# Bias matmuls of the experts in row groups of 32, and rest products by halves

## The reference, cut to what matters

```python
def expert_block(args):
    x_blk, e = args
    gu = x_blk @ w_gate_up[e] + b_gate_up[e]
    g = jnp.minimum(gu[:, :D_FF], SWIGLU_LIMIT)
    u = jnp.clip(gu[:, D_FF:], -SWIGLU_LIMIT, SWIGLU_LIMIT)
    act = (u + 1.0) * (g * jax.nn.sigmoid(SWIGLU_ALPHA * g))
    return act @ w_down[e] + b_down[e]
```

## Time and profile before

| | |
|---|---|
| time, median of 3 | 2289.41 us (2286.81 to 2292.16) |
| profiled execution: time | 2291.37 us |
| profiled execution: span, first to last instruction | 2289.70 us |
| mean granted TensorE clock | 0.982 |
| busy: PE, PE weight loads, DVE, ACT, POOL | 2181.7, 1690.9, 1607.8, 1325.1, 591.0 us |
| read from DRAM, written | 475.30 MB, 43.50 MB |

### The profile page before, as it was taken

How to read it: one execution, slowest core, us unless ns; L and a number is a source line. 1 busy time by engine, 2 the same in 40 slices (tenths; PEclk the granted TensorE clock), 3 DMA queues, 4 the chain that set the end, 5 groups by cost and what they waited for, 6 DMA issues and landing times.

```text
span 2289.7 us, 38734 instructions
## 1 busy us (share of the span) xinstructions
PE 2181.7 (95%) x13724; PEld 1690.9 (74%) x13821; DVE 1607.8 (70%) x1572; ACT 1325.1 (58%) x1484; POOL 591.0 (26%) x538
## 2 busy tenths in 40 slices
PE   7899999999898996999999999999999999999997
PEld 7877777677576874777787777787887777777775
DVE  4065757575466345887887887797998778777777
ACT  4166666666443113566676675676776556555665
POOL 1311101011165001143433432232332223222222
PEclk9999999999999997999999999999999999999998
DMA  4101202121265326998998998898998889888883
GB/s 147 28 28 47 74 26 67 35 67 62 78 206 204 111 84 261 358 344 280 339 347 286 337 353 280 309 375 298 403 368 296 294 294 337 277 291 287 307 313 113
DMA packets 267764, 515.66 MB, mean 225 GB/s; under 512 B 33541, under 2 KB 78032, under 8 KB 267692
## 3 DMA queue, kind: packets, MB, share of 16 engines
q1 hardware_dynamic: 241388, 471.38, 57.2%
q0 software_dynamic: 17088, 39.14, 7.3%
q10 hardware_dynamic: 9216, 4.20, 0.6%
HBM read 475.30 MB, written 43.50 MB: 227 GB/s over the span
## 4 chain that ended last, share of the span: by engine, by line
PE 57%; ACT 2%; DVE 1%; issue 1%; DMA 0%; POOL 0%; POOLq 0%; ACTq 0%; DVEq 0%
PE ex_gu L2112 30%; PE ex_yp L2160 15%; PE ex_rest L2134 4%; PE ex_rest L2177 3%; ACT ex_whi L1732 2%; PE ex_gu L2070 1%; PE ex_gu L2103 1%; PE ex_tr L2078 1%; PE ex_gu L2078 1%; PE ex_yp L2149 0%; DVE ex_wlo L1988 0%; PE ex_rest L2128 0%; PE ex_gu L2086 0%; PE ex_tr L2070 0%; DMA ex_xg<-xn_s,ex_idx 0%
## 5 line engine op out<-in xcount | busy, mean ns | idle before, releaser
L1988 DVE TENSOR_TENSOR ex_wlo<-ex_raw,ex_whi 128x2048 fp32r<-128x2048 f32 x387 | 876.6, 2291 | 217.2 <-ACT ex_whi L1732 217.2
L1732 ACT ACTIVATE ex_whi<-ex_raw 128x2048 fp32r<-128x2048 f32 x387 | 735.5, 1926 | 220.5 <-PE ex_gu L2112 152.0
L2112 PE MATMUL ex_gu<-ex_whi,ex_xhi 128*128 128x512 f32 x1024 | 290.5, 405 | 1.0 <-DVE ex_xlo L2029 1.0
L2112 PE MATMUL ex_gu<-ex_whi,ex_xlo 128*128 128x512 f32 x1024 | 275.3, 391 | 0.0
L2112 PE MATMUL ex_gu<-ex_wlo,ex_xhi 128*128 128x512 f32 x1024 | 274.6, 390 | 0.0
L2112 PEld LDWEIGHTS ex_gu<-ex_whi,ex_xhi 128*128 128x128 f32 x1024 | 191.8, 189 | 52.4 <-issue 7.4
L2112 PEld LDWEIGHTS ex_gu<-ex_whi,ex_xlo 128*128 128x128 f32 x1024 | 192.8, 188 | 41.6
L2112 PEld LDWEIGHTS ex_gu<-ex_wlo,ex_xhi 128*128 128x128 f32 x1024 | 192.8, 188 | 40.7
L705 POOL TENSOR_TENSOR at_wlo<-at_raw,at_whi 128x1024 fp32r<-128x1024 f32 x29 | 71.7, 2472 | 428.3 <-ACT at_whi L520 428.3
L57 PE MATMUL at_job<-xnT_hi,at_whi 128*128 128x512 f32 x416 | 179.6, 432 | 2.1 <-ACT at_rs L555 2.1
L59 PE MATMUL at_job<-xnT_hi,at_wlo 128*128 128x512 f32 x416 | 165.1, 397 | 0.0
(11 more groups left out here) (309 smaller groups left out, 3658.7 us busy)
## 6 DMA issues: line engine op xcount, KB each, us to landing
ex_raw<-in_w_gate_up_dram SPq DMA_DIRECT2D x512, 512.0 KB, 7.5
ex_raw<-in_w_down_dram SPq DMA_DIRECT2D x256, 512.0 KB, 7.2
at_raw<-in_w_in_dram SPq DMA_DIRECT2D x25, 512.0 KB
gT<-at_gst SPq DMA_DIRECT2D x32, 256.0 KB, 2.2
mg_g<-gT SPq DMA_DIRECT2D x32, 256.0 KB, 4.1
n_x<-in_x_dram SPq DMA_DIRECT2D x8, 512.0 KB, 11.0
y_s<-at_yst ACTq DMA_DIRECT2D x64, 64.0 KB, 1.6
ring<-y_s SPq DMA_DIRECT2D x8, 512.0 KB, 5.4
```

The source lines that it names most:

```text
L1732: nc.scalar.activation(w_hi[:, i % RING, :], raw[:, i % SLABS, :], ACT.Copy).then_inc(hi_d, 1)
L1988: nc.vector.tensor_tensor(w_lo[:, slot, :], raw[:, i % SLABS, :], w_hi[:, slot, :].bitcast(F32), ALU.subtract).then_inc(lo_d, 1)
L2112: mm = nc.tensor.matmul(gu[:, half, h, :], x[:, k, :], w[:, kk, h, :], start=k == 0 and n == 0, stop=k == KD - 1 and n == 2)
```

## The change

- `pieces`, `pick` and `sel` go, and with them GpSimd's copy for each expert. In their place `bias` (128 x 3072, bf16) holds the three pieces of one expert's bias in rows 0 to 2 of each group of 32 rows, four times over; all other rows are zero. SP loads it for each expert with four DMAs (`load_bias`), ahead of the load of slab 9 of that expert.
- Constants set once by GpSimd: `ones`, one in those same twelve rows, and `ones_first`, one in rows 0 to 2 alone.
- Main gate/up bias: four matmuls on the four groups of 32 rows, one for each bank of `gu`, together ahead of slab 2. In the second half's banks they now open the accumulation. The waits `hl_d` and `hh_d` move from slab 4 to slab 2.
- Main down bias: two matmuls on two groups of 32 rows, ahead of slab 8, opening the accumulation.
- Rest bias: the same matmuls in shape and number, from `ones_first` and `bias`; for down they move from slab 10 to the second k tile of slab 8.
- Rest products of gate and up: behind slabs 3 and 7, four slabs each time, in place of two behind every second slab.

```diff
+        bias = sb("ex_bias", [P, 3 * D], BF16)
+        ones = sb("ex_ones", [P, P], BF16)
+        ones_first = sb("ex_ones_first", [P, CAP2], BF16)
...
                 for i in range(SLABS):
                     sp.wait_ge(raw_mm, SLABS * (b - 1) + i + 1)
+                    if i == 9:
+                        load_bias(e)
                     load(i, e)
 
-            sp.dma_start(pieces[:, :], bp_s[:, :]).then_inc(ini, 16)
+            def load_bias(e):
+
+                rows = bp_s[0:3 * NE, 0:3 * D].rearrange("(q e) c -> e q c", q=3)
+                for g in range(Q):
+                    sp.dma_start(bias[g * CAP2:g * CAP2 + 3, :],
+                                 rows[bass.ds(e, 1), :, :].rearrange("e q c -> (e q) c")).then_inc(bias_in[g % 2], 16)
+
             for i in range(2):
                 load(i, 0)
+            sp.wait_ge(ones_d, 4 + Q)
+            load_bias(0)
             sp.wait_ge(x_in, 32)
...
+            nc.gpsimd.memset(bias[:, :], 0.0).then_inc(ones_d, 1)
+            nc.gpsimd.memset(ones[:, :], 0.0).then_inc(ones_d, 1)
+            pool.wait_ge(ones_d, 2)
+            for g in range(Q):
+                nc.gpsimd.memset(ones[g * CAP2:g * CAP2 + 3, :], 1.0).then_inc(ones_d, 1)
+                pool.wait_ge(ones_d, 3 + g)
+            nc.gpsimd.memset(ones_first[:, :], 0.0).then_inc(ones_d, 1)
+            pool.wait_ge(ones_d, 3 + Q)
+            nc.gpsimd.memset(ones_first[0:3, :], 1.0).then_inc(ones_d, 1)
+            pool.wait_ge(ones_d, 4 + Q)
...
-                if not first:
-                    hold(pool, slab_mm, SLABS * b + RING, spare)
-                if first:
-                    pool.wait_ge(ini, 19)
-                nc.gpsimd.tensor_copy(sel[:, :], pick[:, bass.ds(e, 1)].to_broadcast([P, P])).then_inc(sel_d, 1)
...
-                if i == 4:
+                if i == 2:
+                    for n in range(2):
+                        pe.wait_ge(bias_in[n], 32 * b + 32)
                     pe.wait_ge(hl_d, 2 * b + 2)
                     pe.wait_ge(hh_d, 3 * b + 3)
-                if pair_of_k == 2:
-                    if i == 2:
-                        pe.wait_ge(sel_d, b + 1)
-                    for h in range(2):
-                        nc.tensor.matmul(gu[:, half, h, :], sel[:, :],
-                                         bp[:, h * FF + half * HALF:h * FF + (half + 1) * HALF], start=False, stop=False)
+                    for g in range(Q):
+                        h, hf = g % 2, g // 2
+                        mine = slice(g * CAP2, (g + 1) * CAP2)
+                        nc.tensor.matmul(gu[:, hf, h, :], ones[mine, :],
+                                         bias[mine, h * FF + hf * HALF:h * FF + (hf + 1) * HALF], start=hf == 1, stop=False)
...
-                                                  start=k == 0 and n == 0, stop=k == KD - 1 and n == 2)
+                                                  start=half == 0 and k == 0 and n == 0, stop=k == KD - 1 and n == 2)
...
                 if i == 8:
                     pe.wait_ge(y_ev, b + 1)
+                    for nh in range(2):
+                        mine = slice(nh * CAP2, (nh + 1) * CAP2)
+                        nc.tensor.matmul(yp[:, nh, :], ones[mine, :],
+                                         bias[mine, 2 * D + nh * HALF:2 * D + (nh + 1) * HALF], start=True, stop=False)
                     pe.wait_ge(hh_d, 3 * b + 4)
...
-                    if more and i % 2:
-                        gate_up_rest(b, i - 1)
-                        gate_up_rest(b, i)
+                    if more and i % 4 == 3:
+                        for n in range(i - 3, i + 1):
+                            gate_up_rest(b, n)
```

More of the change, by code:

```diff
@@ L1610, in experts @@
         quarter = rt["quarter"]
-        pieces = sb("ex_pieces", [P, 3 * D + NE], BF16)
-        bp, pick = pieces[:, 0:3 * D], pieces[:, 3 * D:3 * D + NE]
-        sel = sb("ex_sel", [P, P], BF16)
+        bias = sb("ex_bias", [P, 3 * D], BF16)
+        ones = sb("ex_ones", [P, P], BF16)
+        ones_first = sb("ex_ones_first", [P, CAP2], BF16)
         xg = sb("ex_xg", [P, D])
@@ L1648, in experts @@
         idx_in, idx2_d, x_in, y_out = sem("idx_in"), sem("idx2_d"), sem("x_in"), sem("e_y_out")
-        mid_d, cur_d, piece_d, sel_d = sem("e_mid"), sem("e_cur"), sem("e_piece"), sem("e_sel")
+        mid_d, cur_d, piece_d = sem("e_mid"), sem("e_cur"), sem("e_piece")
+        ones_d, bias_in = sem("e_ones"), [sem(f"e_bias_in{n}") for n in range(2)]
         spare = sem("spare")
@@ L1889, in body @@
             def body(b, over, first=False, t=None):
-                e = over_expert(pool, b) if over else b
-                if not first:
-                    hold(pool, slab_mm, SLABS * b + RING, spare)
-                if first:
-                    pool.wait_ge(ini, 19)
-                nc.gpsimd.tensor_copy(sel[:, :], pick[:, bass.ds(e, 1)].to_broadcast([P, P])).then_inc(sel_d, 1)
                 if not first:
@@ L1946, in further_table @@
                 cmp = ytok[0:1, 0:MAXOVER * NE].rearrange("p (b e) -> p b e", e=NE)
-                dve.wait_ge(ini, 19)
+                dve.wait_ge(ini, 3)
                 cnt = rt["counts"]
@@ L2127, in gate_up_rest @@
                         c = half * HALF + g * P
-                        nc.tensor.matmul(part(g), sel[:, 0:CAP2],
-                                         bp[:, 0:2 * FF].rearrange("p (h c) -> p h c", h=2)[:, :, c:c + P],
+                        nc.tensor.matmul(part(g), ones_first[:, :],
+                                         bias[:, 0:2 * FF].rearrange("p (h c) -> p h c", h=2)[:, :, c:c + P],
                                          start=False, stop=False)
@@ L2147, in down @@
                     pe.wait_ge(hh_d, 3 * b + 5)
-                    for nh in range(2):
-                        nc.tensor.matmul(yp[:, nh, :], sel[:, :], bp[:, 2 * D + nh * HALF:2 * D + (nh + 1) * HALF],
-                                         start=False, stop=False)
                 marks = []
@@ L2160, in down @@
                             mm = nc.tensor.matmul(yp[:, nh, :], x[:, k, :], w[:, kk, nh * HALF:(nh + 1) * HALF],
-                                                  start=k == 0 and n == 0, stop=k == KD - 1 and n == 2)
+                                                  start=False, stop=k == KD - 1 and n == 2)
                             marks.append(mm)
@@ L2169, in down_rest @@
                     pe.wait_ge(hh_d, 3 * b + 6)
[L2170 to L2173, removed]
                 for kk in range(2):
                     k = 2 * (i - 8) + kk
+                    if k == 1:
+                        for g in range(Q):
+                            nc.tensor.matmul(part(g), ones_first[:, :],
+                                             bias[:, 2 * D + g * XW:2 * D + (g + 1) * XW], start=False, stop=False)
                     for g in range(Q):
```

## The result

The changed kernel takes 2274.36 us (median of 3, 2273.76 to 2276.73) against 2289.41: a ratio of 0.9929, with a 95% interval of 0.9913 to 0.9945. That is 15.1 us less, inside the range and 3.4 us above the forecast. Its profiled execution has a span of 2272.7 us against 2289.7; in it the experts stage begins at 873.64 us against 875.21, so 15.4 of the 17.0 us lie in that stage and 1.6 ahead of it.

What follows compares the result with a forecast made beforehand. TensorE (PE), busy 95% of the span, was taken to bound the kernel. Rest by halves -11.7, biases -9.9 and start +3 sum to -18.6 us, from a median of 2289.41 to about 2271 us; range 2260 to 2284.

Steps and rivals of the forecast that it cites:

- (1): Gate/up rest products: two bursts fewer in each of 18 experts, 0.32 us saved per burst, -11.7 us in all.
- (2): Main gate/up bias at slab 2: four row groups together take 0.57 us instead of 0.91, gaining 0.34 us an expert.
- (3): Down bias at slab 8 in row groups: 0.11 us lost without rest, about 0.03 gained with; with gate/up bias, -9.9 us.
- The attention rows: Attention's matmul pairs on two 64-row groups: they run together, with 0.34 us of switching, taken as price for the biases.
- (4): Each expert's bias load on the SP queue: lands before slab 2 needs it, hidden, costing nothing.
- (5): Raw slabs 0 and 1 in experts with rest: released some 8 us later, but hidden.
- (6): Experts stage start: GpSimd's memsets delay the second gather's issue by 4.0 us and PE's start, +3 us.
- Row groups in turn: Rival at the main biases: row groups run one behind the other, kernel slower at 2302.5 us; chance 0.07.
- a free switch: Rival at the main biases: switching tile shape is nearly free for small bf16 weights, 2252 us; chance 0.10.
- a burst paid in full: Rival at the gate/up rest products: a longer burst pays in full, halves save nothing, 2282.5 us; chance 0.07.
- The late bias: Rival at slab 2 of experts with rest: bias load lands late, 2 us wait each, 2307 us; chance 0.06.
- DVE never took over: Judges the rival that DVE limits experts without rest, so those 14 gain nothing, 2274 us; chance 0.08.

Runs made afterwards that it cites:

- e2: Changed kernel with the gate/up rest products back in four bursts, so only the bias changes remain: 2278.75 us, ratio 0.9950 to the kernel before.
- e11: Changed kernel with main biases as full 128-row matmuls, the wide ones tile allocated last so other buffers stay in place: 2284.83 us, ratio 0.9971 to the kernel before.
- e5: Changed kernel with the gate/up bias in two runs of two row groups, at slabs 2 and 6: 2290.20 us, ratio 1.0005 to the kernel before.
- e4: Changed kernel with all main bias matmuls on one row group, rows 0 to 31: 2300.97 us, ratio 1.0042 to the kernel before.
- e0_after_again: The changed kernel measured once more, unaltered: 2276.13 us, ratio 0.9936 to the kernel before.
- e7: Changed kernel with all eight gate/up rest slabs in one burst behind slab 7: 2347.84 us, ratio 1.0257 to the kernel before.
- e8: Changed kernel with GpSimd's new memsets behind the first gather's issue and the first bias load behind the gather wait: 2274.26 us, ratio 0.9931 to the kernel before.
- e1: Kernel before with only the rest products by halves, biases as before: 2282.50 us, ratio 0.9966 to the kernel before.
- e9: Changed kernel with six main biases at slab 2, memsets behind first gather, bias load before slab 8, rest biases heading bursts: 2269.72 us, ratio 0.9904 to kernel before.
- e3: Changed kernel with main biases as full 128-row matmuls at the same slabs, the wider ones tile shifting later buffers: 2289.33 us, ratio 0.9997 to the kernel before.

## Why the prediction was right, point by point

**What bounds.** Right: PE is busy in all of 47.68 and 36.08 us, and the cycles account for the time. The reading of PE's waits was short by one: the 1.6 us for DVE in expert 2 were there before, and a wait of the same kind costs more in the changed kernel, by the clock.

**(1) Rest by halves: the mis-sized term.** The prediction took 0.32 us for each burst saved, -11.7 us. Alone it gave 0.37 an expert, 6.7 us; on top of the biases (e2 against the changed kernel) 0.25 to 0.28, 4.8 us. The mean over five bursts was the wrong price: the two bursts that went stood ahead of a bf16 bias and of transposes and were cheaper to leave (0.21 at slab 2, 0.29 at slab 6), the two that stayed got dearer (0.43 for 0.36, with 0.04 for the bias in their middle), and with the new biases slab 2's burst would have shared its switch with the row groups.

**(2), (3) Biases in row groups.** -9.9 us forecast. In experts without rest 0.21 for 0.23 forecast. With rest 0.55 alone, or 0.42 if the halves are counted first, for 0.37 forecast. By the order in which they are counted, 11 to 13 us, of which the row groups themselves are 8 to 9 (e11). The attention rows gave the right bill for the group (0.59 for the forecast 0.57). The Trainium skill ("TensorEngine Tiling (Array Packing)", Key Properties) names a drain at a change of tiling mode; the traces agree, with 0.26 us in e5 and 0.36 for the four gate/up biases of the changed kernel. By the 3.07 times that the Trainium skill ("TensorE: Matmul & The Clock Gate", Part 3) gives for four row tiles they would take 0.30 us (an estimate); here the group took 0.33 from its start to the next matmul, which holds a part of the switch, and 0.96 in turn (e4), a factor of 2.9.

**(4) The bias by DMA.** Right for this kernel, with one wait of 0.7 us in e0_after_again's trace and one in e2's, after a run of experts without rest. That the queue ahead decides was right too, and e7 shows how little cover there was.

**(5) Raw slabs free later.** Right: PE has no new wait, and ScalarE's waits for gate/up slabs are 7.8 us between 890 and 1035 us, in the first experts, and none between 1035 and 2250.

**(6) The start.** Forecast +3, measured +0.9 in this trace and up to +2.4 in the others. The issue was late nearly as forecast (3.2 for 4.0); the landing was late by less, and e8 shows that the issue alone does not set it. What does stays open.

Terms as measured: an expert with rest behind one without went from 44.56 to 43.70, which is 0.86, so the cycles give -0.79 x 8 - 0.86 x 10 - 0.21 x 14 = -17.9; start +0.9; expert 2 +1.7, by a wait 0.3 longer and 3.4 us at the lower clock: -15.3, against -15.4 in the stage. So there is luck in how near the total came: (1) was forecast 5 to 7 us too large, the biases 1 to 3 too small, the start some 2 too dear, and the clock in expert 2 was not forecast at all.

**The rivals.** Row groups in turn, a free switch and a burst paid in full are refuted by e4, e5 and e1. The late bias did not come here but is what e7 ran into. DVE never took over in the steady cycles: in e9's 35.66 us without rest PE is busy 35.63.

## What to carry to other kernels

Price a switch of tile shape by the rows on both sides of the very place that changes, not by a mean over all: work of different shapes next to each other shares a switch, so two edits that each remove one do not add up. A small load behind large ones in one queue lands when they do; before moving the release of large buffers, look at what small load is queued behind them, or give it another queue. And keep later buffers where they are when a tile's size changes, or measure the shift by itself.

## What the runs showed of the hardware that was not expected

- Matmul speed depended on where the buffers lie: a shift of 192 bytes a partition made all main matmuls 1% slower (0.916 against 0.907 us for four; e3 and e11), some 7 us of the kernel by its cycles. Each of the two places was traced once, and the other traces of the changed kernel and of before all have 0.907; which of the shifted operands does it wasn't tried.
- A short wait can cost as much again by the clock, and its length alone does not decide. In e7, behind a wait of 3.7 us, PE's matmuls ran at the lower level (four in 1.87 us); behind one of 2.9 us, at 1444.98, they did not. In expert 2 of the changed kernel the clock fell behind 2.0 us of wait, and so it did in e0, e2 and e5; in e8, behind 1.99 us at the same place, it stayed full. What decides isn't shown by these runs.
